# Two rounded weight buffers instead of three, and the split of the panel two ahead moved behind the current panel's eviction

## What is computed

```python
for layer in range(DEPTH):                       # DEPTH = 2
    p_l = split_columns(modulate(rms_norm(x, norm1), sh1, sc1) @ w_in)     # w_in: 1024 x 10768
    p_c = split_columns(modulate(rms_norm(ctx, norm1), csh1, csc1) @ w_in)
    ym  = mlstm_output(mlstm_bidirectional(...), p[3], mlstm_norm)         # 4 heads, chunked
    ya  = attention(rope(rms_norm(q)), rope(rms_norm(k)), v)               # 8 heads, 2 kv heads
    yc  = gate_b * conv3(gate_c * u)
    merged = sum(sigmoid(gate_b) * (y_b @ w_proj_b))                       # three branches
    x = x + g1 * (merged @ w_out)
    x = x + g2 * (square(relu(modulate(rms_norm(x, norm2), sh2, sc2) @ w_up)) @ w_down)
    ...                                          # the same for ctx in layer 0
return rms_norm(x, final_norm)
```

## Time and profile before

| | |
|---|---|
| median of 3 runs | 1846.35 us (1844.9 to 1846.6) |
| the profiled execution | 1847.76 us |
| its span, first to last instruction | 1846.0 us |
| TensorE busy | 1820.1 us, 99% of the span |
| VectorE, ScalarE, GpSimd busy | 57%, 37%, 8% |
| mean granted TensorE clock | 0.997 of full speed |
| packets of the main DMA queue, share of 16 engines' span | 40.7% |

### The profile page before, as it was taken

How to read it: one execution, slowest core, us unless ns; L and a number is a source line. 1 busy time by engine, 2 the same in 40 slices (tenths; PEclk the granted TensorE clock), 3 DMA queues, 4 the chain that set the end, 5 groups by cost and what they waited for, 6 DMA issues and landing times.

```text
span 1846.0 us, 24597 instructions
## 1 busy us (share of the span) xinstructions
PE 1820.1 (99%) x10059; PEld 1546.9 (84%) x10059; DVE 1048.2 (57%) x1538; ACT 689.1 (37%) x951; POOL 155.1 (8%) x160
## 2 busy tenths in 40 slices
PE   7999999999999999999999999999999999999998
PEld 4887788778888888878888888788998899999997
DVE  5436634544556665467666656554547656566555
ACT  3425533323222222243232223343644444445444
POOL 2100100001110101320000000301100110020000
PEclk9999999999999999999999999999999999999999
DMA  9221122121443453625444536132132375575653
GB/s 326 97 91 46 46 91 68 48 69 46 139 149 123 137 183 114 227 86 189 137 137 137 175 118 187 53 130 92 61 123 92 115 228 183 183 229 167 193 188 114
DMA packets 214287, 245.52 MB, mean 133 GB/s; under 512 B 5836, under 2 KB 186400, under 8 KB 214176
## 3 DMA queue, kind: packets, MB, share of 16 engines
q1 hardware_dynamic: 213872, 243.85, 40.7%
q10 hardware_dynamic: 304, 0.10, 0.0%
HBM read 242.89 MB, written 1.05 MB: 132 GB/s over the span
## 4 chain that ended last, share of the span: by engine, by line
PE 93%; DVE 2%; ACT 1%; issue 1%; POOL 0%; DVEq 0%; ACTq 0%; POOLq 0%
PE pp L1178 19%; PE pp L1182 19%; PE pp L1179 19%; PE pp L1186 4%; PE pp L1185 4%; PE pp L1187 4%; PE pc L1375 3%; PE pp L1109 2%; PE pp L1110 2%; PE pp L1111 2%; PE pc L1069 2%; PE pc L1070 2%; PE pc L1068 2%; PE pc L1465 1%; PE pc L1427 1%; PE pc L1282 1%
## 5 line engine op out<-in xcount | busy, mean ns | idle before, releaser
L1908 DVE TENSOR_TENSOR wL<-raw,wH 128x1024 fp32r<-128x1024 f32 (+1 forms) x360 | 452.4, 1297 | 236.5 <-ACT wH L1482 233.6
L1178 PE MATMUL pp<-hH,wH 128*128 128x512 f32 (+1 forms) x1708 | 571.0, 345 | 0.6 <-ACT hH L1691 0.3
L1179 PE MATMUL pp<-hH,wL 128*128 128x512 f32 (+1 forms) x1708 | 561.2, 339 | 0.0
L1482 ACT ACTIVATE wH<-raw 128x1024 fp32r<-128x1024 f32 x360 | 360.4, 1050 | 303.0 <-PE pp L1187 103.5
L1182 PE MATMUL pp<-hL,wH 128*128 128x512 f32 (+1 forms) x1708 | 439.6, 339 | 1.4 <-POOL hL L1845 0.8
L1178 PEld LDWEIGHTS pp<-hH,wH 128*128 128x128 f32 x1708 | 324.2, 190 | 43.9 <-issue 9.0
L1179 PEld LDWEIGHTS pp<-hH,wL 128*128 128x128 f32 x1708 | 324.1, 190 | 35.8 <-issue 1.7
L1182 PEld LDWEIGHTS pp<-hL,wH 128*128 128x128 f32 x1708 | 294.6, 190 | 37.6 <-POOL hL L1845 1.7
L1178 PE MATMUL pp<-yH,wH 128*128 128x512 f32 (+1 forms) x320 | 115.3, 367 | 0.0
L1185 PE MATMUL pp<-yH,wH 128*128 128x512 f32 (+1 forms) x320 | 114.4, 357 | 0.0
L1186 PE MATMUL pp<-yL,wH 128*128 128x512 f32 (+1 forms) x320 | 114.4, 357 | 0.0
(11 more groups left out here) (270 smaller groups left out, 2225.0 us busy)
## 6 DMA issues: line engine op xcount, KB each, us to landing
raw<-in_w_in SPq DMA_DIRECT2D x83, 1024.0 KB, 5.2
raw<-in_w_up SPq DMA_DIRECT2D x32, 1024.0 KB, 5.5
raw<-in_w_down SPq DMA_DIRECT2D x32, 1024.0 KB, 5.1
pair_W<-in_w_ada SPq DMA_DIRECT2D x10, 2048.0 KB, 8.1
ada_Y<-in_w_ada SPq DMA_DIRECT2D x10, 1024.0 KB, 11.8
ada_H<-in_w_ada SPq DMA_DIRECT2D x8, 1024.0 KB, 10.9
raw<-in_w_proj_m SPq DMA_DIRECT2D x8, 1024.0 KB, 5.1
raw<-in_w_proj_a SPq DMA_DIRECT2D x8, 1024.0 KB, 5.2
```

Source lines behind the costliest of these rows:

```text
L1178: pe.matmul(dsts[b], wh[b], hi[:, kt, ts_], start=first, stop=False)
L1179: pe.matmul(dsts[b], wl[b], hi[:, kt, ts_], start=False, stop=False)
L1482: act.activation(wH[:, p % HIGH, a:a + KH, :], raw[:, p % RAW, a:a + KH, :], ACT.Copy).then_inc(wH_ready, 1)
L1908: dve.tensor_tensor(wL[:, p % RAW, ks, :], raw[:, p % RAW, ks, :], wH[:, p % HIGH, ks, :].bitcast(F32), ALU.subtract).then_inc(wL_ready, 1)
```

## The change

The constant `HIGH` goes from 3 to 2, which makes `wH` two buffers of 1 MB instead of three. The wait in ACT's `split` then is for panel p - 2 instead of p - 3. The calls of `split` for the panel two ahead move, on ACT and on DVE, from the head of a panel's step to its end. Nothing else differs: the order of the list, the instructions themselves and the four raw buffers stay.

```diff
-HIGH = 3
+HIGH = 2
...
                 elif k == "panel":                       # ScalarE, and the same on VectorE
                     nx = next_panel(st)
-                    if nx:
-                        split(nx)
                     kind, p, c_, b_ = st["kind"], st["p"], st["c"], st["b"]
...
                         y_high(no, y_tmp[:, :, ts_], slice(2 * c_, 2 * c_ + 2), ts_)
+                    if nx:
+                        split(nx)
                 elif k == "squares":
```

## The result

The changed kernel takes 1911.9 us (median of 4 runs, 1906.7 to 1912.2) against 1846.5 for the kernel before beside it. The ratio is 1.0346, with a 95% interval of 1.0333 to 1.0359. The forecast was 1890.8, its range 1868 to 1908: the direction was right, the size 21 us too small, and the time lies 4 us above the range.

What follows compares the result with a forecast made beforehand. TensorE, busy 99%, was taken as the bound. Waits of 23.3 + 9.8 + 3.25 + 5.1 - 0.2 = 41.25 us plus 3.2 for the clock added 44.45, giving 1890.8 us against the median; range 1868 to 1908.

Steps and rivals of the forecast that it cites:

- clock term: One half-clock stretch of 3.2 us behind each of the two longest rotary waits, 1.6 us lost each: +3.2 us.
- rotary, layer 0: TensorE waits at `qrot` j = 2, +6.5 us; behind the fourth `aq`, +3.2; behind the first `gate`, +1.85.
- rotary, layer 1: The same three places in layer 1: +5.6 us, including 0.45 from `qrot` j = 0, then +3.05 and +3.1.
- heads: Attention heads behind `gate` and `proj` panels in both layers, where splits delay `scores` or `probs`: 9.8 us together.
- norms: Three norms, where ACT splits before the first squares: +1.05, +1.0 and +1.2, together 3.25 us.
- modulation rows: DVE's row copies come behind its split, +2.2 and +2.4 us; with two weighted sums, 5.1 together.
- mLSTM and merge: Small steps +0.7 and +0.4 us, earlier evictions in layer 0 -0.4, layer 1's last merge -0.9: sum -0.2.
- last panel: Wait before the final panel: given no term in the forecast, so 0.
- Plain panels: Splits finish before the next panel needs them, with 1.5 us to spare in layer 1's `up`: cost 0.
- rival 1: Clock falls at all six waits above 2.3 us, 9.6 us instead of 3.2: 1897.2 us, chance 0.14.
- Rivals 2, 3 and 4: Only long waits appear, 1872.4, chance 0.12; layer 1's panels lose cover, 1930, 0.07; not slower, small-step waits hidden, 1845, 0.05.

Runs made afterwards that it cites:

- pair of one-engine kernels: Against the kernel before, three buffers kept: only ACT's split moved behind its eviction (not in cu, cb, up), 1889.5 us; only DVE's moved, 1852.8 us.
- order-alone kernel: Kernel before with its three buffers, but the split behind the panel's own eviction as in the changed kernel: 1898.2 us, 1.0291.
- second profile: The changed kernel itself measured and profiled once more, nothing altered: 1910.7 us, 1.0346; profiled span 1904.3 us.
- filled kernels: Throwaway matmuls put into waits: two waits of the kernel before with two splits moved, 1862.6 us; eight waits of the changed kernel, 1902.8 us.
- two-wait kernel: Kernel before, three buffers and old order, except splits of panels 18 and 108 put ahead of `qrot` j = 2 in each layer: 1864.4 us, 1.0099.

## Why the prediction was too low

The step that failed is the clock term: "I add one such stretch to each, +3.2". TensorE was busy 19.1 us longer. That is 16 of the missing 21 us. Of the rest, 2.5 are the last panel and 2.3 the merge and the mLSTM, and smaller misses partly cancel. The terms against the traces, in us:

| term | foretold | measured |
|---|---|---|
| rotary, layer 0 | 6.5, 3.2, 1.85 | 6.7, 1.9, 2.0 |
| rotary, layer 1 | 5.6, 3.05, 3.1 | 6.6 (0.9 of it at `qrot` j = 0), 1.5, 3.2 |
| heads | 9.8 | 10.4 |
| norms | 3.25 | 3.1 |
| modulation rows | 5.1 | 4.8 |
| mLSTM and merge | -0.2 | 2.1 |
| last panel | 0 | 2.5 |
| clock | 3.2 | 19.1 |

The waits sum to 44.8 of the 45.3 us by which TensorE's idle time grew, and the forecast had 41.25.

**Plain panels** cost nothing, as foretold, in either layer.

**Rotary, heads, norms, modulation rows: right.** Their sum was foretold as 41.45 and came out as 40.2. The two long waits were hit to 0.2 us in layer 0 and 1.0 in layer 1. The middle one was priced too high in both layers, 3.1 for some 1.7. The prediction put 1.2 us of DVE's split in front of L2309, as what frees bank 3. But what releases TensorE is the bare semaphore at L2307, just ahead of it. DVE's queue raised it while the second half of the split still ran: TensorE goes on at 317.64, the split ends at 318.73. The changed kernel:

```profile
316.37 2.36 DVE L1908 TENSOR_TENSOR wL<-raw,wH 128x1024 fp32r<-128x1024 f32 x2 [14.69 <-ACT wH L1482]
317.64 1.16 PE L1417 MATMUL pc<-q_a,con 128*128 128x256 f32 x4 [1.96 <-DVEq L2307]
```

The prediction named the eviction, ACT's split and DVE's split as one chain. The pair of one-engine kernels shows which link decides: ACT's. For the norms the amount was right, and the cause as I put it ("now ACT splits first") left open which edit does it. It is the missing buffer, not the order.

**mLSTM and merge: sign wrong.** What failed here is "the last merge of layer 1 is evicted earlier, -0.9". The eviction is earlier. But the same change of order moved three roundings of the merged rows behind ACT's split, and GpSimd behind them. The changed kernel, ACT, then GpSimd and DVE:

```profile
1671.25 0.60 ACT L1561 ACTIVATE gs<-pp 128x512 f32<-128x512 f32 x1 [3.69 <-PE pp L1182]
1672.02 2.01 ACT L1482 ACTIVATE wH<-raw 128x1024 fp32r<-128x1024 f32 x2 [0.17 <-ACT gs L1561]
1673.93 1.66 ACT L1778 ACTIVATE hH<-merged 128x512 fp32r<-128x512 f32 x3
```

```profile
1674.62 4.51 POOL L1881 TENSOR_TENSOR hL<-merged,hH 128x512 fp32r<-128x512 f32 x3 [7.07 <-ACT hH L1778]
1679.09 2.28 POOL L1817 TENSOR_TENSOR merged<-merged,gs 128x512 f32<-128x512 f32 x1
1678.16 4.28 DVE L1908 TENSOR_TENSOR wL<-raw,wH 128x1024 fp32r<-128x1024 f32 x2 [0.46 <-ACT wH L1482]
```

In the kernel before, ACT rounded these rows directly behind L1563. GpSimd was free when the last product came. Now it comes to it 1.4 us late and takes 2.28 us for it instead of 1.29, beside two halves of DVE's split that take 4.28 instead of 2.36. The merge cost some 1.0 us where the prediction had -0.9. I costed the eviction alone and did not follow the queues that it feeds.

**The last panel: missed.** The prediction gave the missing buffer no price of its own. In the plain panels that was right. But the wait for "panel p - 2" is a count that the closing panel 177 does not raise, and I read it as that panel's end. The three norms belong here too, though their waits were foretold under another cause: the order-alone kernel and the changed one differ by 10 us by the ratios.

**The clock: mechanism right, size far off.** The two longest waits, for which the 3.2 us stood, cost 4.4: TensorE worked 4.1 and 4.7 us at half clock there, for the rest of each 10.2 us stretch it stood still. What the prediction put at nothing are the stretches everywhere else. Ten of 3.4 us lie on work and cost 1.7 each. Four of them stand at the waits of 2 to 3 us of rival 1, 6.8 us; one at the modulation row of layer 0 and two in layer 1 (1427.9, 1683.9) with no wait above 1 us just ahead, 5.1; three are the norms', 5.1 for the 3.2 that the kernel before lost in two. That makes 18.2 in all. Rival 1 had the right mechanism, and I gave it a chance of 0.14. In this execution the clock did fall at all six of its waits, for 11.2 us where it had 9.6. It missed the others. Which of the short stretches come differs between executions (9 instead of 12 in the second profile), so the 19.1 is this execution's.

The filled kernels show that it is the emptiness of the long waits: behind a filled wait the granted clock stays at 1.00 in the windows where it was 0.50. (The Trainium skill, "TensorE: Matmul & The Clock Gate", section "What's actually happening", has activity release the throttle; the filled waits agree, with 1.00 where it was 0.50.) The runs leave open which wait of 1 to 3 us will be followed by a stretch, and why this differs between executions.

**Rivals 2, 3 and 4** did not happen: the short waits came nearly at their size, there is no `wL` wait in the plain panels, and no small step is hidden. The signs that the prediction named came: 96% for "about 97%", waits of 6.5 and 6.0 at L1417, 1.6 before `scores`, 1.9 at L1309, 2.0 at L1267, 5.76 for a plain panel. Of the three waits of 3 us at bank 3 one came at 3.0, two only at 2.0.

## What to carry to other kernels

When work that prepares a later stage moves behind the current stage's end, look at what each engine's queue does next: in plain stretches the move is free, and the whole price is paid where a latency chain follows (here 27 of 178 calls carried three quarters of it). A ring with one buffer less needs its work placed behind such chains, not in front, and every wait on a count has to be read at the places where the count does not rise. Price the clock with the waits: a wait of 6 us cost 6 us and 2 to 2.5 more behind it, and the many waits of 2 to 3 us cost up to 1.7 more each.

## What the chip showed that I had not expected

- In waits of 6.5 and 6.0 us with thin steps around them the clock fell within 0.5 us of their start, for 10.2 us that reached 4.1 and 4.7 us behind them; in the two-wait kernel for 10.2 and 6.8, from 1.5 and 4.0 us into the wait. Stretches of 3.4 us stood behind waits of 2 to 3 us (1421.0, 1728.2).
- The same kernel, profiled twice, had 12 and 9 such stretches, in part at other places, and spans of 1910.4 and 1904.3 us. Between its runs the time varied from 1906.1 to 1912.8.
- Matmuls whose result is thrown away held the clock at its high level through a wait and the panel behind it, at no cost in time where they ended inside the wait: by the traces 4.7 us less behind two waits, by the ratios 7 us over the whole kernel with eight waits filled.
- GpSimd and DVE's split lengthened each other, in these rows always the one that began second. GpSimd's addition of 128x512 took 1.29 us alone and 2.28 when it began inside the split. When it began first it took 1.30, and the two halves 3.13 instead of 2.36. Beside an addition of 128x1024 (2.40 us, as alone) one half took 3.41 instead of 1.22.
- DVE's queue raised a bare semaphore (L2307) while the instruction ahead of it still ran. TensorE, which waited for it, went on at 317.64, 1.1 us before DVE's split ended.
